# Weighted values with the value block stationary in the first attention of a decoder layer, and its changed entry

## The reference

```python
c = jnp.cumsum(jax.nn.log_sigmoid(f_logit.astype(jnp.float32)), axis=1)
...
for i in range(S // Q_BLOCK):
    q0, q1 = i * Q_BLOCK, (i + 1) * Q_BLOCK
    s = jnp.einsum('bqhd,bkhd->bhqk', q[:, q0:q1], k[:, :q1]) * scale
    bias = c[:, :, q0:q1, None] - c[:, :, None, :q1]
    causal = (q0 + jnp.arange(Q_BLOCK))[:, None] >= jnp.arange(q1)[None, :]
    s = jnp.where(causal[None, None], s + bias, -jnp.inf)
    p = jax.nn.softmax(s, axis=-1)
    outs.append(jnp.einsum('bhqk,bkhd->bqhd', p, v[:, :q1]))
```

## Time and profile before

| | us |
|---|---|
| median of 3 runs (lowest, highest) | 2770.1 (2766.78, 2772.87) |
| profiled execution | 2776.75 |
| its span, first to last instruction | 2774.9 |
| first scores of the attention loops start | 95.97 |
| the phase behind the attention starts | 404.8 |
| PE busy over the whole span | 2598.7 (94%) |
| DVE, ACT, POOL busy | 2251.6, 912.4, 1309.0 |

### The profile page before, as it was taken

How to read it: one execution, slowest core, us unless ns; L and a number is a source line. 1 busy time by engine, 2 the same in 40 slices (tenths; PEclk the granted TensorE clock), 3 DMA queues, 4 the chain that set the end, 5 groups by cost and what they waited for, 6 DMA issues and landing times.

```text
span 2774.9 us, 45831 instructions
## 1 busy us (share of the span) xinstructions
PE 2598.7 (94%) x17059; PEld 1687.8 (61%) x17251; DVE 2251.6 (81%) x4526; ACT 912.4 (33%) x1606; POOL 1309.0 (47%) x864
## 2 busy tenths in 40 slices
PE   8999979999988877899999999999999999999996
PEld 3677646689977765555565565565564564664653
DVE  4244556658789999788989988988998999999998
ACT  3333334521125556432222232232232322331324
POOL 2110010000034442266766766766666677676772
PEclk9999989999999999999999999999999999999998
DMA  4000212320103355999999999999999999999995
GB/s 165 24 16 17 84 61 98 131 99 14 38 22 130 133 209 220 326 382 361 359 353 382 355 355 351 365 373 354 347 375 356 365 373 372 345 380 367 348 342 208
DMA packets 277917, 690.68 MB, mean 249 GB/s; under 512 B 29896, under 2 KB 112328, under 8 KB 273488
## 3 DMA queue, kind: packets, MB, share of 16 engines
q0 software_dynamic: 110592, 402.70, 38.6%
q1 hardware_dynamic: 167120, 285.25, 29.0%
HBM read 626.99 MB, written 60.88 MB: 248 GB/s over the span
## 4 chain that ended last, share of the span: by engine, by line
PE 27%; DVE 19%; DMA 15%; issue 12%; POOL 3%; ACT 1%; SPq 1%; DVEq 0%; ACTq 0%; POOLq 0%
PE h_psum L1748 9%; DMA early<-u_blocks 6%; PE o_psum L2228 6%; PE r_t_psum L1211 5%; PE g_psum L2228 4%; DVE early L2069 3%; DMA early<-v_blocks,pick_index 3%; DVE rt_hot L1647 3%; POOL early L1755 2%; DMA early<-v_blocks 2%; PE h_psum L1261 2%; DVE wide L2073 2%; DMA early<-u_rows,pick_index 2%; DMA fetched<-u_rows,pick_index 1%; DVE early L1738 1%
## 5 line engine op out<-in xcount | busy, mean ns | idle before, releaser
L1748 PE MATMUL h_psum<-early 128*128 128x384 bf16 x5496 | 767.3, 300 | 6.6 <-DVE early L1738 3.4
L1748 PEld LDWEIGHTS h_psum<-early 128*128 128x128 bf16 x5496 | 537.7, 98 | 234.3 <-issue 10.1
L1755 POOL DMA_INDIRECT early<-u_rows,pick_index x320 | 456.9, 1428 | 227.8 <-DVE dots L2069 142.3
L1755 POOL DMA_INDIRECT early<-v_blocks,pick_index x320 | 459.5, 1436 | 199.3 <-DVE wide L2073 117.3
L2228 PE MATMUL o_psum<-v_split,w_split 128*128 128x512 bf16 x2293 | 543.0, 382 | 1.6 <-issue 0.2
L2073 DVE SCALAR_TENSOR_TENSOR wide<-early,dots,wide 128x1024 f32<-128x1024 f32 x320 | 405.5, 1279 | 23.5 <-DMA early<-v_blocks,pick_index 22.0
L2069 DVE CUSTOM_DVE_ANT_0 early<-early,wide 128x1024 f32<-128x1024 f32 x320 | 386.9, 1218 | 30.3 <-DMA early<-u_rows,pick_index 27.5
L2228 PEld LDWEIGHTS o_psum<-v_split,w_split 128*128 128x128 bf16 x2304 | 227.2, 99 | 277.2 <-issue 9.1
L2228 PE MATMUL g_psum<-v_split,w_split 128*128 128x512 bf16 x1399 | 348.8, 384 | 35.6 <-DVE w_split L2035 12.6
L2228 PEld LDWEIGHTS g_psum<-v_split,w_split 128*128 128x128 bf16 x1536 | 150.0, 98 | 198.0 <-issue 31.1
L1947 ACT ACTIVATE v_split<-early 128x512 bf16<-128x512 f32 x256 | 159.0, 622 | 320.9 <-PE o_psum L2228 217.5
(11 more groups left out here) (230 smaller groups left out, 3335.1 us busy)
## 6 DMA issues: line engine op xcount, KB each, us to landing
early<-v_blocks SPq DMA_DIRECT2D x256, 256.0 KB, 6.4
early<-u_blocks SPq DMA_DIRECT2D x115, 512.0 KB, 8.4
gates<-wide SPq DMA_DIRECT2D x20, 2048.0 KB, 6.4
gate<-gates SPq DMA_DIRECT2D x31, 1280.0 KB, 21.4
early<-w_query SPq DMA_DIRECT2D x8, 1024.0 KB, 5.9
rt_u_pre<-u_blocks SPq DMA_DIRECT2D x13, 512.0 KB, 4.0
early<-w_fox SPq DMA_DIRECT2D x4, 1536.0 KB, 6.4
early<-u_rows,pick_index POOLq DMA_INDIRECT x320, 8.3
```

The source lines that it names most:

```text
L1748: mm = pe.matmul(bank(half)[:, 0:width * P], u_split[:, k, part, c], xs[:, first:first + width, xpart, c, :], start=(c == 0 and part == 0 ...
L1755: pool.indirect_dma_start(row, None, source, bass.IndirectOffsetOnAxis(ap=pick_index[:, tile, at:at + 1], axis=0)).then_inc(arrived, 16)
```

## The change

- Values: v's block is stationary (128 keys x 64 columns) and the turned probabilities are streamed, 128 columns. The output comes turned already, [64, 128], so the flip goes. The two heads of a pair are written to partitions 0 to 63 and 64 to 127 of one bank, one after the other for each key block: `values` runs once for two units.
- The probabilities are divided by their sum in SBUF, over the whole length of the unit, before the turn (`normalise`); `scale_out` goes. `turn` waits for `normed`.
- Entry: the forget logits ride as 8 more columns with the second attention's values (`VF` = 136 columns, three tiles to a bank). They come by rows, get bias and log-sigmoid as 128 x 64, and are turned to [8, 1024] by eight transposes for the scan. c_row is stored to memory and loaded again into all partitions by eight DMAs (`neg_c_rows`), which replaces the `minus_row` products; its sign is turned in c_col instead. The first pair's projection has two banks in turn.

The diff, cut to its core:

```diff
+VF = P + FOX_HEADS
+VF_TILES = 3
...
-        w_kv = (probs[:, 2:4].rearrange("p j n -> p (j n)").bitcast(BF16)
-                .rearrange("p (h j c n) -> p h j c n", h=2, j=2, c=KD))
-        f_tmp = [buffer[0:FOX_HEADS] for buffer in (q_t[1], k_t[1], v_rows[1].rearrange("p t c -> p (t c)"))]
+        w_k = (probs[:, 2].bitcast(BF16).rearrange("p (h c n) -> p h c n", h=2, c=KD))
+        w_vf = (pair_out[:, :, :, :].rearrange("p k h n -> p (k h n)")[:, 0:2 * KD * VF]
+                .rearrange("p (h c n) -> p h c n", h=2, c=KD))
...
-        o_psum = ctx.enter_context(nc.psum_tensor("a_o_psum", [P, 2, P], F32))
+        o_psum = ctx.enter_context(nc.psum_tensor("a_o_psum", [P, P], F32))
...
+            return t_psum[1] if pair == 0 and chunk % 2 else p_psum
...
+                sp.wait_ge(first_ready, 2)
+                sp.dma_start(neg_c_rows, c_row).then_inc(c_stored, 16)
+                sp.wait_ge(c_stored, 16)
+                for h in range(FOX_HEADS):
+                    sp.dma_start(neg_c[:, h], neg_c_rows[h].partition_broadcast(P)).then_inc(bias_in[int(h >= 2)], 16)
...
-                        mm = products(t_psum[t // 4][:, t % 4 * P:t % 4 * P + P],
-                                      lambda a: xt[:, a, c, t * P:(t + 1) * P], lambda b: w_kv[:, b, 1, c],
+                        mm = products(vf_psum[t // VF_TILES][:, t % VF_TILES],
+                                      lambda a: xt[:, a, c, t * P:(t + 1) * P], lambda b: w_vf[:, b, c],
                                       c == 0, c == KD - 1)
...
                 pe.wait_ge(first_ready, 1)
-                for h in range(FOX_HEADS):
-                    if h == 1:
-                        pe.wait_ge(first_ready, 2)
-                    if h >= 2:
-                        pe.wait_ge(bcast_copied, h - 1)
-                    for half in range(2):
-                        mm = pe.matmul(s_psum[h % 2][:, half], minus_row[:, h], c_row[:, half * 512:half * 512 + 512],
-                                       start=True, stop=True)
-                    mm.then_inc(bcast_done, 1)
-                    project_fox(0, 0, 2 * KD + h * KD // 2, 2 * KD + (h + 1) * KD // 2)
-                pe.wait_ge(raw_copied, 3)
+                for t in range(TILES):
+                    mm = pe.transpose(s_psum[1][0:FOX_HEADS, t // 4, t % 4 * P:t % 4 * P + P], f_rows[:, t], ident)
+                mm.then_inc(first_made, 1)
+                pe.wait_ge(first_copied, 7)
+                project_fox(0, 0, KD, FOX_CHUNKS * KD)
+                pe.wait_ge(first_ready, 2)
                 for t in range(TILES):
                     mm = pe.transpose(t_psum[0][:, t * FOX_HEADS:(t + 1) * FOX_HEADS], c_row[:, t * P:(t + 1) * P],
                                       ident[0:FOX_HEADS, 0:FOX_HEADS])
-                mm.then_inc(bcast_done, 1)
+                mm.then_inc(first_made, 1)
...
                 def turn(pair, u):
                     qb, n = query_block(pair, u), UNITS * pair + u
-                    pe.wait_ge(exp_done, n + 1)
+                    pe.wait_ge(normed, n + 1)
...
-                def values(pair, kp, u):
-                    qb, hh, n = query_block(pair, u), u % 2, UNITS * pair + u
-                    if u == 0:
+                def values(pair, kp, m):
+
+                    qb, n = query_block(pair, 2 * m), TILES * pair + m
+                    if m == 0:
                         pe.wait_ge(chunk_copied, FOX_CHUNKS * pair + FOX_CHUNKS)
-                    pe.wait_ge(turn_copied, n + 1)
+                    pe.wait_ge(turn_copied, 2 * (n + 1))
                     if past(n):
-                        pe.wait_ge(out_scaled, n)
-                    if hh == 0 and past(n):
-                        pe.wait_ge(flip_copied, TILES * pair + u // 2)
-                    cols = slice(HEAD_DIM * hh, HEAD_DIM * hh + HEAD_DIM)
+                        pe.wait_ge(out_copied, n)
                     for b in range(qb + 1):
-                        mm = pe.matmul(o_psum[:, 0, cols], probs_t[:, u % 2, b * P:(b + 1) * P],
-                                       v_rows[kp][:, b, cols], start=(b == 0), stop=(b == qb))
+                        for hh in range(2):
+                            dims = slice(HEAD_DIM * hh, HEAD_DIM * hh + HEAD_DIM)
+                            mm = pe.matmul(o_psum[dims, :], v_rows[kp][:, b, dims],
+                                           probs_t[:, hh, b * P:(b + 1) * P], start=(b == 0), stop=(b == qb))
                     mm.then_inc(pv_done, 1)
-
-                def flip_fox(pair, u):
-                    pe.wait_ge(out_scaled, UNITS * pair + u)
-                    flip()
...
+                        if u % 2 == 0 and u >= 2:
+                            values(pair, kp, u // 2 - 1)
+                        elif u == 0 and past(pair):
+                            values(pair - 1, 1 - kp, TILES - 1)
                         turn(pair, u)
-                        if u >= 1:
-                            values(pair, kp, u - 1)
-                        elif past(pair):
-                            values(pair - 1, 1 - kp, UNITS - 1)
...
-                def scale_out(pair, u):
-                    hh, n = u % 2, UNITS * pair + u
-                    cols = slice(HEAD_DIM * hh, HEAD_DIM * hh + HEAD_DIM)
+                def normalise(pair, u):
+                    n, length = UNITS * pair + u, (query_block(pair, u) + 1) * P
                     dve.wait_ge(exp_done, n + 1)
                     dve.reciprocal(row_sum[:, u % PROBS, 0:1], row_sum[:, u % PROBS, 0:1]).then_inc(inv_done, 1)
-                    dve.wait_ge(pv_done, n + 1)
                     dve.wait_ge(inv_done, n + 1)
-                    dve.tensor_scalar(o_rows[:, cols], o_psum[:, 0, cols], row_sum[:, u % PROBS, 0:1], None,
-                                      ALU.mult).then_inc(out_scaled, 1)
+                    dve.tensor_scalar(probs[:, u % PROBS, 0:length], probs[:, u % PROBS, 0:length],
+                                      row_sum[:, u % PROBS, 0:1], None, ALU.mult).then_inc(normed, 1)
...
+                        if u + 1 < UNITS:
+                            normalise(pair, u + 1)
+                        elif not last:
+                            normalise(pair + 1, 0)
...
-                        act.wait_ge(pv_done, n - 1)
+                        act.wait_ge(pv_done, (n - u % 2) // 2)
```

More of the change, by code:

```diff
@@ L440, in attend @@
                     if last:
-                        values(pair, kp, UNITS - 1)
-                        flip_fox(pair, UNITS)
-                pe.wait_ge(bcast_copied, FOX_HEADS + 1)
+                        values(pair, kp, TILES - 1)
                 scores(0, 0, 0)
@@ L518, in bias_and_max @@
                     head = 2 * pair + hh
+                    if u == 0 and pair < 2:
+                        dve.wait_ge(bias_in[pair], (32, 96)[pair])
                     dve.wait_ge(scores_done, n + 1)
@@ L637, in _ @@
-                act.wait_ge(fa_step, 1)
-                act.activation(f_tmp[2], f_tmp[2], ACT.Ln, bias=1.0).then_inc(fa_step, 1)
-                act.wait_ge(first_made, 2)
-                act.activation(raw[:, :], s_flat[1], ACT.Copy).then_inc(raw_copied, 1)
-                act.wait_ge(first_made, 3)
-                for k in range(2):
-                    act.activation(sv_rows[:, 4 * k:4 * k + 4].rearrange("p t c -> p (t c)"), t_psum[k][:, :],
-                                   ACT.Copy).then_inc(raw_copied, 1)
@@ L645, in _ @@
[L645 to L654 removed]
+                        act.wait_ge(w_first_in, 16)
@@ new lines, in _ @@
+                for k, bank in enumerate(vf_psum):
+                    tiles = slice(VF_TILES * k, min(VF_TILES * (k + 1), TILES))
+                    act.activation(f_rows[:, tiles], bank[:, 0:tiles.stop - tiles.start, P:VF], ACT.Copy
+                                   ).then_inc(first_copied, 1)
+                for k, bank in enumerate(vf_psum):
+                    tiles = slice(VF_TILES * k, min(VF_TILES * (k + 1), TILES))
+                    act.activation(sv_rows[:, tiles], bank[:, 0:tiles.stop - tiles.start, 0:P], ACT.Copy
+                                   ).then_inc(first_copied, 1)
@@ L655, in _ @@
+                act.wait_ge(f_step, 4)
+                act.activation(f_tmp, f_tmp, ACT.Exp).then_inc(f_step, 1)
+                act.wait_ge(f_step, 5)
+                act.activation(f_tmp, f_tmp, ACT.Ln, bias=1.0).then_inc(f_step, 1)
+                for chunk in range(FOX_CHUNKS):
+                    copy_chunk(0, 0, chunk)
+                act.wait_ge(first_made, 5)
                 act.activation(c_col[:, :, :].rearrange("p t h -> p (t h)"), t_psum[0][:, 0:TILES * FOX_HEADS],
-                               ACT.Copy).then_inc(bcast_copied, 1)
+                               ACT.Copy, scale=-1.0).then_inc(first_copied, 1)
```

197 lines of the change are left out of this document (84 added, 113 removed).

## The result

| | before | after |
|---|---|---|
| median, us (runs; lowest, highest) | 2767.2 (8; 2765.4, 2776.5) | 2740.1 (8; 2735.9, 2763.4) |
| profiled execution | 2776.75 | 2763.42 |
| first scores of unit 0 of pair 0 | 95.97 | 68.05 |
| four pairs, scores of unit 0 to the next | 64.15, 68.74, 68.74, 107.21 | 64.48, 72.13, 68.68, 105.50 |
| next phase | 404.81 | 378.84 |

The medians differ by 27 us, against 32 forecast; the ratio of the means is 0.9913, with a 95% interval of 0.9884 to 0.9942, so the change is faster. What lies behind the attention took 2370.1 us of the span in the profile before and 2382.8 in this one, with the same instructions; the profiled execution is 23 us above its own median.

The account below looks back on a forecast made before the run. PE was taken to pace the attention until 390 us. Entry -25.2, pairs 0 to 2 -11.1, fourth pair -4.9 and POOL +9.5 gave -31.7: 2776.75 to 2745, or 2738 as a median; range 2724 to 2769 us.

Parts of the forecast that it names:

- Entry: Before the first scores: forget projection and broadcast matmuls go, wider matmuls and forget turns are added; -25.2 us on PE.
- Values 0.11 for a head and a block: Value matmuls in column halves: 0.11 us per head and key block, as in the scores' row halves, against 0.229 before.
- A: Rival for the values: column halves take turns, 0.22 us per head and block; total -4.5, 2766 us; chance 0.20.
- B: Rival for the values: weight load and stream don't overlap, 0.33 us per head and block; +24, 2794 us; chance 0.07.
- The weight-load rule: Skill's rule for value matmuls: loads overlap running matmuls only where row groups differ; cited for slower values, not leaned on.
- The gain of 8.2 a pair: PE time saved per head pair by cheaper values and dropped flips, less a fixed 0.18 us per group.
- The new wait: Last four units of pairs 0 to 2: PE waits for the division in DVE's order, 4.5 us a pair.
- the sum for pairs 0 to 2: Attention, first three pairs: saved values and flips against the wait for the division, 3 x (-8.2 + 4.5) = -11.1 us.
- POOL: Weight casts and subtractions on POOL hold DVE's division, at the first stall and end of pair 0; +9.5 us (1 to 16).
- the first stall: First division beside POOL's cast and subtraction: PE waits 1.2 us if it gets in between, else 6.6; 5.5 taken.
- Fourth pair: Last head pair: -8.2 for values and flips, +2.3 waits behind rope, +1.0 POOL stalls; -4.9 us.
- the tail: Fourth pair after the projection: scale, flip and hand-overs go, division and a POOL stall come; 0 us.

Follow-up runs that it names:

- e8_heads: Changed kernel with all value records of head 0 ahead of those of head 1, not by turns; one run, 2769.3 us.
- e13_shares: Changed kernel with projection pieces moved behind unit 14 and ahead of unit 15 in pairs 0 to 2; 2734.8 us, 0.9880 of before.
- e3_order: Changed kernel with each unit's division behind the next unit's bias and maximum on DVE; 2764.9 us, 1.0004 of before.
- e9_between: Changed kernel with reciprocal and division between the next unit's bias and maximum on DVE; 2745.0 us, 0.9958 of before.
- e12_even: Changed kernel with only the even units' division between the next unit's bias and maximum; 2739.7 us, 0.9891 of before.
- e4_pool: Changed kernel with POOL's cast and subtraction of the weights cut into pieces of 512 columns; 2736.6 us, 0.9891 of before.
- e2_loops: Kernel before with only the new values, division and flips, keeping the old entry; 2778.2 us, 1.0039 of before.

## Why the prediction was right, and where not

- Entry, -25.2 forecast, -27.9 measured. The forget projection gave 13.0, not 11: the next part began at 21.92, not 23.8. I held x's last low halves at the old 17.39; they start at 16.70. And the projection's 36 records took 7.94, 0.22 each and not 0.25, and left next to no backlog. The loads of the bias didn't wait: SP issued them from 56.12, as estimated, and bias(0) began at 68.85, right behind the scores.
- Values 0.11 for a head and a block: right; each further block of both heads adds 0.21 to 0.22. A (0.22) and B (0.33) are refuted, and e8_heads shows what A would look like. The weight-load rule that I had set beside B (the Trainium skill, TensorE: Matmul & The Clock Gate, Part 3) would have halves of the same rows not overlap their loads. Here it does not hold: alternating, the streams alone (two at once, 0.107 each) fill the 0.22, and head by head a record takes 0.108, which is the stream without its load.
- The gain of 8.2 a pair was right for the values and flips, which took 17.7 from start to next start in pair 2 before and 9.1 in e13_shares: 8.6 less. But PE's busy time there is only 6.1 less (67.12 to 61.04, at full clock), since 2.5 came back elsewhere. The turn between values in column halves and scores in row halves takes 0.12 to 0.15 more to the next start (eight blocks 1.02 from 259.78, 0.90 before), eight times a pair; the rest is mostly the latency of the last record ahead of each wait, which counts as busy.
- The new wait, +4.5 a pair: in pair 2 of the kernel after, idle time on PE rose by 4.2, in the places named (the values behind copies 2.1, the turn of unit 15 1.5). The place and size hold. That it comes from DVE's order held less: e3_order and e9_between made DVE's idle time smaller and PE's waits longer, e12_even gained 0.9 at one place, and e13_shares took the wait of unit 15 away by giving PE something to do.
- The failed step is the sum for pairs 0 to 2, "3 x (-8.2 + 4.5)": measured, without POOL, -0.1 for pair 2 in place of -3.7. It is 2.1 of gain that came back in other PE records, and 1.8 of clock (62.83 busy, 61.04 in e13_shares), which I had priced at nothing: behind the 1.5 us wait the turns took 1.81 in place of 1.09 and five 512-column records 2.01 in place of 1.24. In e4_pool, where the clock stayed up, pair 2 is -1.7.
- POOL, +9.5: the mechanism is shown (e4_pool, e2_loops), the sizes depend on luck. At the first stall PE waited 0.9 in the profile after and 6.2 in e2_loops, where I had 1.2 or 6.6 and took 5.5. The wait at the end of pair 0 was 4.4, with the slower clock behind it, but with POOL in pieces 2.3 of it stayed, so POOL's hold is half of it and not all. Pairs 0 and 1 together were +3.7 against +2.1 forecast: the first stall too dear, the clock and the missing gain left out.
- Fourth pair, -4.9 forecast, -1.7 measured: PE waits 7.5 for divisions there, where I had 3.3. The 2.3 in the projection is right (0.81, 0.19 and 1.24); the other 5.2 are two waits in the tail, ahead of 367.64 and 371.79, beside POOL's four subtractions on w_out (a division of 256 columns took 1.72 there, 0.35 at 362.12), and I had put the tail at nothing.

That the forecast of 2738 met 2740 is luck in part: an entry undervalued by 2.7 stood against loops overvalued by 8.5, and this series of before had a median 3 lower than the one I started from.

## What to carry to other kernels

When a change takes work off the bounding engine and adds a link to the chain that it waits for, ask first what that engine can do in the meantime: the saved time came back only when independent matmuls were moved to where the wait is. An emptier engine elsewhere is worth nothing if the result comes later. And price a wait with the clock that may fall behind it: two waits that look like 1.5 and 4.4 us cost 3.0 and 6.4, the slower records counted, while the same wait of 1.5 cost no more than itself in e4_pool. A sum over stages can hide this: e12_even came out at +0.2 from parts of -2.5 and +2.2.

## What the hardware showed that I had not expected

- Column halves run side by side only if neighbouring records use different halves: 0.055 us a record, against 0.108 head by head and 0.122 on the whole array. In all three the next weight load is hidden, or nearly so: a stream of 128 columns alone takes 0.107.
- Behind a wait of 1.49 us for a turn the clock fell in two kernels (after, e2_loops) and stayed up in a third (e4_pool); behind one of 4.43 it was at 1.2 GHz from 137 to past 141.
- A division of 128 columns, 0.29 us by itself, took 0.29 or 5.93 at the same place of two programs, as it came just before or just after POOL's next instruction.
